# Attention software pipeline one unit deeper, bias and gate passes on GpSimd, and a second MLP that ends in token order with its residual in the accumulators

## The chip, the cores and the metric

The kernel runs on one core of a Trainium2 chip. The metric is the device time of one execution in microseconds, taken as the median of the runs shown. The profile comes from one further execution, whose span runs from its first to its last instruction.

## The reference, cut to what matters

One sequence of 256 tokens with width 1024 passes through two blocks. The first has gated linear attention, a sliding-window attention with eight heads (swa), an output product and an expert layer (PEER). The second has two layers. Only the parts around the change are shown:

```python
h = rmsnorm(x, g_attn[0]); x = x + dsa_mixer(h, rel_bias, ...)   # 8 heads, keys chosen by an indexer
x = x + sq_relu_mlp(rmsnorm(x, g_mlp[0]), w_up[0], w_down[0])
kv_shared = shared_kv(x, ...)
h = rmsnorm(x, g_attn[1]); x = x + nsa_mixer(h, rel_bias, kv_shared, ...)  # 8 heads, 3 gated branches
x = x + sq_relu_mlp(rmsnorm(x, g_mlp[1]), w_up[1], w_down[1])
return rmsnorm(x, g_final)

def sq_relu_mlp(h, w_up, w_down):                 # 1024 -> 4096 -> 1024
    return jnp.square(jax.nn.relu(h @ w_up)) @ w_down
```

In `dsa_mixer` the logits of a head are scores plus a relative bias plus a mask of the chosen keys. In `nsa_mixer` the softmax rows of the second and the third branch are multiplied by a sigmoid gate per token, head and branch before they meet the values.

## The kernel before, in words

**Layout.** Activations are held transposed: feature chunks of 128 on the partitions, 256 tokens along the free dimension (`XT`, eight chunks). Weights come as 488 slots of 128 x 1024 fp32 (512 KB each) through a ring of four, which SP refills when `slots_used` says that a slot is free (L369 to L374). Most slots are used in a split form: ScalarE writes a rounded high part (`split_high`, L337 to L343), VectorE or GpSimd the remainder into the slot's own place (`split_low`, L345 to L351), and a product is three fp32r matmuls, high x high, high x low and low x high (`three`, L525 to L529).

**The attentions.** `attention_units` (L94 to L99) lists 16 units for swa, 16 for dsa and 32 for nsa (two branches a head). Units of the first token tile (`tt` = 0) have 128 keys, those of the second 256. Each engine has its own `attend`, an in-order program over steps. TensorE in a step issues `scores(step)`, `transposes(step - 2)`, `products(step - 3)` (L634 to L640; L606, L615, L631). ScalarE issues `exps(st)`, `copies(st - 2)`, `outs(st - 4)` (L1064 to L1070). VectorE issues `logits(st)` (bias add and row maximum, L1407 and L1410) and then `normed(st - 1)` (reciprocal L1415 and a scaling L1419, in nsa with the gate, L1421). The buffers hold four units of scores and probabilities (`u % 4`) and two of transposed probabilities and of outputs (`u % 2`). For dsa the bias is two adds in a row on VectorE, the second waiting for the first: the relative bias `Bt` (L1834), then the mask `selb` (L1835). GpSimd does nothing in these stages, but for memsets (L422) and weight loads beside swa. In swa VectorE also has a filler, a row of the modulation of 128 x 1024 (L1442), in every second step.

**What comes between two score products.** `products(u)` waits for `att_copied` of its own unit and for `att_out` of the output two before it. Both are set by ScalarE in the iteration before, behind that iteration's `exps`, and `exps` waits for the row maximum of its own unit.

**The MLPs.** `mlp` (L897 to L915) works in rounds of eight slots: four up slots (L531; 24 matmuls of 128 x 256 into `pu`), which VectorE evacuates with relu (L1850) and ScalarE squares, then four down slots (`down_slot`, L567; 24 matmuls with the weights as the stationary side, 256 tokens moving, into `pacc`). The accumulators are opened by eight small matmuls with zeros (`open_acc`, L811), and closed in the same way (`close_acc`, L817). The expert layer's value product uses another form, `token_slot` (L576 to L587): the activations are stationary and 512 columns of weights move, 12 matmuls for a slot (L584 to L586), tokens on the partitions.

**The head of the second MLP.** Its first slot (`raw_slot`, L543) runs on the unnormalised stream. The sum of squares is made by GpSimd (L465) and TensorE (L558), ScalarE takes the root, VectorE the reciprocal (L1588), and only then can relu free the two `pu` entries.

**The tail.** After the last down slot: `close_acc`, the residual add on VectorE over 128 x 2048 (L1971), squares on ScalarE, a sum over the partitions by eight fp32 matmuls (`norm_sum("fin2")`, L517), root, reciprocal over 128 x 256 (L1392), eight scalings (L1394), and one store of 1 MB (L377), whose landing ends the kernel. Output leaves in feature order.

## Time and profile before

| | us |
|---|---|
| runs shown | 1850.57, 1854.89, 1855.41 |
| median | 1854.89 |
| profiled execution, its own time | 1855.27 |
| span of that execution | 1853.7 |
| TensorE busy | 1682.4 (91% of the span) |
| VectorE busy | 1069.6 (58%) |
| ScalarE busy | 835.0 (45%) |
| GpSimd busy | 448.0 (24%) |
| mean granted TensorE clock | 0.935 of full speed |

Matmul records are pipelined and their ends modelled, so neighbouring records overlap: the pace is the distance of their starts. A matmul with fp32 operands stands as two records (passes). In timeline rows the first number is the start, the second the length of a run of equal instructions, and the brackets hold the idle time before it and what ended that. Nearly all activations of ScalarE stand under L1006, a helper.

### The profile page before, as it was taken

The numbers are of one execution on the slowest core, as the hardware profiler recorded it, in microseconds if no ns is written. First come the engines' busy times: TensorE is split into PE (matmuls) and PEld (weight loads), VectorE is DVE, ScalarE is ACT, GpSimd is POOL, SyncE is SP. The second block draws the span as 40 slices with busy tenths as digits, with TensorE's granted clock in tenths as the row PEclk, the third lists the DMA queues.
The fourth block names the chain that finished last, engine by engine and source line by source line (L and its number), as shares of the span: only waits on it lengthen the run. The fifth ranks groups of instructions, "written<-read, shape, count | busy, mean of one in ns | idle before, by whom it ended". The sixth has DMA issues, their size and how long they took to land.

```text
span 1853.7 us, 34170 instructions
## 1 busy us (share of the span) xinstructions
PE 1682.4 (91%) x11384; PEld 1517.6 (82%) x11384; DVE 1069.6 (58%) x2448; ACT 835.0 (45%) x1767; POOL 448.0 (24%) x399
## 2 busy tenths in 40 slices
PE   5975889999999999999999977589999988899996
PEld 3872789998999999778887755479999848699996
DVE  5537569916777732555555542666555624765554
ACT  3214445565444445555555531355555403555553
POOL 4102367886666677000000010000000000010000
PEclk8975899999999999999999987699999987999999
DMA  8851234553444445555555531125555462045552
GB/s 312 326 187 46 78 128 149 178 177 127 141 136 138 145 159 181 192 190 190 190 191 191 191 128 46 45 81 170 182 182 182 145 216 91 1 154 183 184 182 91
DMA packets 80752, 287.63 MB, mean 155 GB/s; under 512 B 10080, under 2 KB 11408, under 8 KB 80432
## 3 DMA queue, kind: packets, MB, share of 16 engines
q1 hardware_dynamic: 72016, 257.30, 42.0%
q0 software_dynamic: 7344, 26.35, 3.8%
q10 hardware_dynamic: 1328, 3.15, 0.5%
q8 instruction: 38, 0.62, 0.1%
q14 instruction: 26, 0.21, 0.0%
HBM read 284.14 MB, written 2.62 MB: 155 GB/s over the span
## 4 chain that ended last, share of the span: by engine, by line
PE 83%; DVE 9%; ACT 3%; issue 2%; DMA 2%; POOL 1%; SPq 0%; DVEq 0%; ACTq 0%; POOLq 0%
PE pu L527 12%; PE pu L528 12%; PE pu L529 12%; PE pacc L586 6%; PE pacc L584 6%; PE pacc L585 6%; PE pacc L527 3%; PE pacc L528 3%; PE pacc L529 3%; PE pu L499 3%; PE pu L509 2%; PE pacc L631 2%; PE pm L800 2%; PE pn L800 2%; PE pn L517 1%
## 5 line engine op out<-in xcount | busy, mean ns | idle before, releaser
L343 ACT ACTIVATE ring_hi<-ring 128x512 fp32r<-128x512 f32 x880 | 505.6, 622 | 524.6 <-PE pu L529 288.1
L350 DVE TENSOR_TENSOR ring_lo<-ring,ring_hi 128x512 fp32r<-128x512 f32 x592 | 386.0, 694 | 336.4 <-ACT ring_hi L343 336.2
L527 PE MATMUL pu<-Xh,ring_hi 128*128 128x256 f32 x1472 | 431.0, 293 | 23.7 <-DVE Xl L1382 5.3
L528 PE MATMUL pu<-Xl,ring_hi 128*128 128x256 f32 x1472 | 419.6, 285 | 0.0
L529 PE MATMUL pu<-Xh,ring_lo 128*128 128x256 f32 x1472 | 419.3, 285 | 0.0
L350 POOL TENSOR_TENSOR ring_lo<-ring,ring_hi 128x512 fp32r<-128x512 f32 x288 | 370.2, 1307 | 130.8 <-ACT ring_hi L343 130.1
L527 PEld LDWEIGHTS pu<-Xh,ring_hi 128*128 128x128 f32 x1472 | 285.1, 194 | 30.2 <-issue 18.1
L528 PEld LDWEIGHTS pu<-Xl,ring_hi 128*128 128x128 f32 x1472 | 285.8, 194 | 0.2
L529 PEld LDWEIGHTS pu<-Xh,ring_lo 128*128 128x128 f32 x1472 | 285.2, 194 | 0.0
L584 PE MATMUL pacc<-ring_hi,vh 128*128 128x512 f32 x512 | 200.5, 392 | 0.0
L586 PE MATMUL pacc<-ring_lo,vh 128*128 128x512 f32 x512 | 200.5, 392 | 0.0
L585 PE MATMUL pacc<-ring_hi,vl 128*128 128x512 f32 x512 | 199.7, 390 | 0.0
L527 PE MATMUL pu<-X2h,ring_hi 128*128 128x256 f32 x512 | 145.8, 285 | 2.7 <-DVE big L1850 2.7
L527 PE MATMUL pacc<-act_h,ring_hi 128*128 128x256 f32 x512 | 144.9, 283 | 0.0
L528 PE MATMUL pacc<-act_l,ring_hi 128*128 128x256 f32 x512 | 144.9, 283 | 0.0
L529 PE MATMUL pacc<-act_h,ring_lo 128*128 128x256 f32 x512 | 144.9, 283 | 0.0
L528 PE MATMUL pu<-X2l,ring_hi 128*128 128x256 f32 x512 | 144.9, 283 | 0.0
L529 PE MATMUL pu<-X2h,ring_lo 128*128 128x256 f32 x512 | 144.8, 283 | 0.0
L584 PEld LDWEIGHTS pacc<-ring_hi,vh 128*128 128x128 f32 x512 | 96.0, 187 | 33.1 <-issue 5.5
L586 PEld LDWEIGHTS pacc<-ring_lo,vh 128*128 128x128 f32 x512 | 96.1, 188 | 21.1
L585 PEld LDWEIGHTS pacc<-ring_hi,vl 128*128 128x128 f32 x512 | 96.3, 188 | 16.1
L465 POOL TENSOR_TENSOR R<-sq 128x256 f32<-128x256 f32 x2 | 1.5, 744 | 430.0 <-ACT sq L1006 430.0
(328 smaller groups left out, 2619.0 us busy)
## 6 DMA issues: line engine op xcount, KB each, us to landing
ring<-in_weights SPq DMA_DIRECT2D x488, 512.0 KB, 3.3
big<-in_ada POOLq DMA_DIRECT2D x40, 512.0 KB, 6.2
bias_row<-big ACTq DMA_DIRECT2D x1, 1536.0 KB, 6.8
XT<-in_xT ACTq DMA_DIRECT2D x1, 1024.0 KB, 8.4
scr<-in_ada POOLq DMA_DIRECT2D x2, 512.0 KB, 12.4
tk<-in_ada POOLq DMA_DIRECT2D x2, 512.0 KB, 14.1
early_h<-in_ada POOLq DMA_DIRECT2D x2, 512.0 KB, 16.2
early_l<-in_ada POOLq DMA_DIRECT2D x2, 512.0 KB, 17.7
```

The source lines that it names most:

```text
L343: nc.scalar.activation(ring_hi[:, n % 2, half], ring[:, n % RING, half], ACT.Copy).then_inc(s["split_hi"], 1)
L350: api.tensor_tensor(ring_lo[:, n % RING, half], ring[:, n % RING, half], ring_hi[:, n % 2, half], ALU.subtract).then_inc(s[LOW[name][0]], 1)
L499: last = mm(entry(e), slot(n)[:, c * P:(c + 1) * P], rhs[:, c, :], start=(c == 0), stop=(c == C - 1))
L509: last = mm(entry(e)[:, tt * P:(tt + 1) * P], lhs[:, c, tt * P:(tt + 1) * P], slot(n)[:, c * P:(c + 1) * P], start=(c == 0), stop=(c == C ...
L527: mm(out, ring_hi[:, n % 2, w], xh, start=start, stop=False, skip_group_check=True)
L528: mm(out, ring_hi[:, n % 2, w], xl, start=False, stop=False, skip_group_check=True)
L529: return mm(out, ring_lo[:, n % RING, w], xh, start=False, stop=stop, skip_group_check=True)
L584: mm(out, xh[:, rows], ring_hi[:, n % 2, w], start=False, stop=False, skip_group_check=True)
L585: mm(out, xl[:, rows], ring_hi[:, n % 2, w], start=False, stop=False, skip_group_check=True)
L586: last = mm(out, xh[:, rows], ring_lo[:, n % RING, w], start=False, stop=False, skip_group_check=True)
L631: last = mm(out, v, p, start=(k == 0 and UNITS[u][4]), stop=(k == len(pairs) - 1 and UNITS[u][5]))
L800: last = mm((pm, pn)[k % 2][:, i * P:(i + 1) * P], sq[:, j // 2, j % 2 * P:(j % 2 + 1) * P], scr[:, j * P:(j + 1) * P], start=True, stop=True)
```

## The change

1. TensorE issues transposes three and products four units behind the scores; ScalarE's copies and outputs move by one step too. This holds for all three attentions.
2. dsa: GpSimd adds `Bt` and `selb` into the score buffer ahead of time (16 adds, up to four units ahead), and VectorE then has one add in place of two.
3. nsa: GpSimd multiplies the 32 probability tiles by reciprocal and gate; VectorE only makes the reciprocal.
4. Second MLP: down slots run as `token_slot`. In place of `open_acc`, 16 fp32 matmuls of 128 x 128 against the identity (`residual_rows`) bring the residual stream into the accumulators in token order, after the fourth up slot. The last slot finishes token tile 0 before token tile 1; there is no `close_acc`.
5. Tail: per token tile one Square with a row sum, a root of 128 x 1, a reciprocal of 128 x 1, two scalings of 128 x 512 against the gain row, and a store of 256 KB for each half. `norm_sum("fin2")` is gone. The gain row is loaded by GpSimd's queue (512 KB, one row to all partitions) at the start of the second MLP.

```diff
@@ sync
-            sp.wait_ge(s["out_ready"], 1)
-            sp.dma_start(out_d, sq[:, :, :].rearrange("p a b -> p (a b)")).then_inc(s["out_stored"], 16)
-            sp.wait_ge(s["out_stored"], 16)
+            for i in range(2 * TT):
+                sp.wait_ge(s["out_ready"], i + 1)
+                sp.dma_start(out_d[:, i * 512:(i + 1) * 512], out_rows[:, i // 2, i % 2 * 512:(i % 2 + 1) * 512])\
+                    .then_inc(s["out_stored"], 16)
+            sp.wait_ge(s["out_stored"], 16 * 2 * TT)
@@ gpsimd
+            u0, u1 = SPAN["dsa"]
+            for u in range(u0, u1):
+                tt, h = UNITS[u][1:3]
+                L = keys_of(u)
+                pool.wait_ge(s["chosen"], tt + 1)
+                if u >= u0 + 4:
+                    pool.wait_ge(s["att_exp"], u - 3)
+                nc.gpsimd.tensor_tensor(Sb[:, u % 4, 0:L], Bt[:, h, T - L:T], selb[:, tt, 0:L], ALU.add)\
+                    .then_inc(s["att_prebias"], 1)
             add_squares("mlp0")
+            pool.wait_ge(s["gates_done"], 1)
+            for u in range(*SPAN["nsa"]):
+                _, tt, h, b = UNITS[u][:4]
+                pool.wait_ge(s["att_inverse"], u + 1 - SPAN["nsa"][0])
+                pr = Pb[:, u % 4, 0:keys_of(u)]
+                nc.gpsimd.tensor_scalar(pr, pr, stats[:, 8 + u % 4:9 + u % 4], gates[:, tt, 3 * h + 1 + b:3 * h + 2 + b],
+                                        ALU.mult, ALU.mult).then_inc(s["att_normed"], 1)
             add_squares("mlp1")
+            pool.wait_ge(s["slots_used"], SLOT["mlp1"])
+            pool.dma_start(fin_row[:, :], fin_row_d.partition_broadcast(P)).then_inc(s["weights_row_loaded"], 16)
@@ tensor, attend
-                for step in range(u0, u1 + 3):
+                for step in range(u0, u1 + 4):
                     if step < u1:
                         scores(step)
-                    if u0 <= step - 2 < u1:
-                        transposes(step - 2)
                     if u0 <= step - 3 < u1:
-                        products(step - 3)
+                        transposes(step - 3)
+                    if u0 <= step - 4 < u1:
+                        products(step - 4)
@@ tensor, mlp
+            def down(name, k, g):
+                done = 0 if name == "mlp0" else FF // P
+                pe.wait_ge(s["act_tiles"], tick(g, 4, done + k // BODY * 4 + k % 4 + 1))
+                if name == "mlp0":
+                    down_slot(name, k, act_h[:, k % 4, :], act_l[:, k % 4, :], g)
+                else:
+                    token_slot(name, k, act_h[:, k % 4, :], act_l[:, k % 4, :], g)
+            def residual_rows(product):
+                for c in range(C):
+                    pe.wait_ge(s["evacs"], USE[product] + c + 1)
+                    for tt in range(TT):
+                        at0 = tt * D + c * P
+                        mm(paccf[:, at0:at0 + P], XT[:, c, tt * P:(tt + 1) * P], ident[:, :], start=(c % 4 == 0), stop=False,
+                           skip_group_check=True)
+            def last_rows(name, k):
+                n = SLOT[name] + k
+                for tt in range(TT):
+                    rows = slice(tt * P, (tt + 1) * P)
+                    xh, xl = act_h[:, k % 4, rows], act_l[:, k % 4, rows]
+                    for half, w in enumerate(halves):
+                        out = paccf[:, tt * D + half * 512:tt * D + (half + 1) * 512]
+                        split_ready(name, k, half, None)
+                        mm(out, xh, ring_hi[:, n % 2, w], start=False, stop=False, skip_group_check=True)
+                        mm(out, xl, ring_hi[:, n % 2, w], start=False, stop=False, skip_group_check=True)
+                        last = mm(out, xh, ring_lo[:, n % RING, w], start=False, stop=True, skip_group_check=True)
+                    last.then_inc(s["rows_done"], 1)
             def mlp(name):
-                open_acc()
...
+                if name == "mlp0":
+                    open_acc()
                 raw_slot(name, lambda c: None)
                 one_sum(name)
                 for k in range(1, 4):
                     up_slot(name, k, USE[name] + k, None, 4, None, raw_x[name])
-                four_down(None)
-                with pe.Fori(1, FF // P // 4) as g:
+                if name == "mlp1":
+                    residual_rows("b_o")
+                for k in range(4, 8):
+                    down(name, k, None)
+                with pe.Fori(1, FF // P // 4 - (name == "mlp1")) as g:
...
+                    for k in range(k0 + 4, k0 + 7):
+                        down(name, k, None)
+                    pe.wait_ge(s["act_tiles"], 2 * FF // P)
+                    last_rows(name, k0 + 7)
...
-            norm_sum("fin2")
@@ scalar, attend
-                for st in range(u0, u1 + 4):
+                for st in range(u0, u1 + 5):
                     if st < u1:
                         exps(st)
-                    if u0 <= st - 2 < u1:
-                        copies(st - 2)
-                    if u0 <= st - 4 < u1:
-                        outs(st - 4)
+                    if u0 <= st - 3 < u1:
+                        copies(st - 3)
+                    if u0 <= st - 5 < u1:
+                        outs(st - 5)
@@ scalar, tail
-            act.wait_ge(s["x_ready"], 4)
-            squares(XT[:, :, :], sq[:, :, :])
-            root(NORM["fin2"])
+            act.wait_ge(s["roots"], NORM["mlp1"])
+            for tt in range(TT):
+                act.wait_ge(s["rows_done"], tt + 1)
+                f(scratch[:, tt, :], paccf[:, tt * D:(tt + 1) * D], ACT.Square,
+                  accum_out=stats[:, tt:tt + 1]).then_inc(s["row_squares"], 1)
+                act.wait_ge(s["row_squares"], tt + 1)
+                f(stats[:, 4 + tt:5 + tt], stats[:, tt:tt + 1], ACT.Sqrt, scale=1.0 / D, bias=eps[:, 0:1])\
+                    .then_inc(s["row_roots"], 1)
@@ vector
+                    inverse = v.reciprocal(stats[:, 8 + u % 4:9 + u % 4], stats[:, 4 + u % 4:5 + u % 4])
+                    if kind == "nsa":
+                        inverse.then_inc(s["att_inverse"], 1)
+                        return
...
             def dsa_bias(u, S, ps):
-                step(v.tensor_tensor(S, ps, Bt[:, h, T - L:T], ALU.add))
-                v.tensor_tensor(S, S, selb[:, tt, 0:L], ALU.add).then_inc(s["att_biased"], 1)
+                dve.wait_ge(s["att_prebias"], u - SPAN["dsa"][0] + 1)
+                v.tensor_tensor(S, ps, S, ALU.add).then_inc(s["att_biased"], 1)
...
-            dve.wait_ge(s["acc_done"], 3)
-            v.tensor_tensor(XT[:, :, :], pacc[:, :, :], XT[:, :, :], ALU.add).then_inc(s["x_ready"], 1)
-            dve.wait_ge(s["x_ready"], 4)
-            scaled(sq, XT, [column("fin2", c) for c in range(C)], NORM["fin2"]).then_inc(s["out_ready"], 1)
+            def rows_out(tt):
+                dve.wait_ge(s["row_roots"], tt + 1)
+                step(v.reciprocal(stats[:, 8 + tt:9 + tt], stats[:, 4 + tt:5 + tt]))
+                for half in halves:
+                    v.scalar_tensor_tensor(out_rows[:, tt, half], paccf[:, tt * D + half.start:tt * D + half.stop],
+                                           stats[:, 8 + tt:9 + tt], fin_row[:, half], ALU.mult, ALU.mult)\
+                        .then_inc(s["out_ready"], 1)
+            dve.wait_ge(s["weights_row_loaded"], 16)
+            rows_out(0)
+            rows_out(1)
```

## Rows read from the trace of the kernel before

**Rows 1.** The page, part 4: shares of the chain that ended last.

```profile
PE 83%; DVE 9%; ACT 3%; issue 2%; DMA 2%; POOL 1%; SPq 0%; DVEq 0%; ACTq 0%; POOLq 0%
```

**Rows 2.** Windows (span; busy PE, PEld, DVE, ACT, POOL; PEclk; DMA): swa, second MLP.

```profile
160.00:198.00 38.00, 33.85 (x98) 17.74 (x98) 30.70 (x100) 16.61 (x65) 10.34 (x13) 0.52 0.17 56
...
1660.00:1833.00 173.00, 173.00 (x1444) 173.00 (x1442) 96.55 (x179) 86.53 (x178) 0.00 (x0) 1.00 0.53 174
```

**Rows 3.** Timeline of the tail.

```profile
1833.04 1.05 PE L817 MATMUL pacc<-zeros 128*128 128x256 bf16 x8
1834.13 2.29 DVE L1971 TENSOR_TENSOR XT<-pacc,XT 128x2048 f32<-128x2048 f32 x1 [4.63 <-PE pacc L817]
1836.45 1.91 ACT L1006 ACTIVATE sq<-XT 128x2048 f32<-128x2048 f32 x1 [7.76 <-DVE XT L1971]
1838.41 5.29 PE L517 MATMUL pn<-sq,ones 128*128 128x256 f32 x16 [4.33 <-ACT sq L1006]
...
1846.11 3.26 DVE L1394 SCALAR_TENSOR_TENSOR sq<-XT,cols,R 128x256 f32<-128x256 f32 x8
1849.39 0.36 SPq L377 DMA_DIRECT2D outT<-sq  x1
```

**Rows 4.** DMA issues (KB each, us from issue to landing): the store, and a small load.

```profile
big<-bias_row POOLq DMA_DIRECT2D x8, 128.0 KB, 2.4
...
outT<-sq SPq DMA_DIRECT2D x1, 1024.0 KB, 3.9
```

**Rows 5.** Line L584, token-order product (ns min/median/max, first and last start).

```profile
L584 PE MATMUL pacc<-ring_hi,vh x512: 387/389/474, 735.3 to 1086.1; 128*128 128x512 f32 x171
```

**Rows 6.** Timeline of TensorE, end of nsa: ten fp32 passes of 128 x 128.

```profile
1616.82 1.35 PE L631 MATMUL pacc<-big 128*128 128x128 f32 x10
```

**Rows 7.** Timeline of the head of the second MLP.

```profile
1648.74 1.28 ACT L1006 ACT_TABLE_LOAD   x1
...
1654.32 0.39 PE L527 MATMUL pu<-X2h,ring_hi 128*128 128x256 f32 x1 [1.35 <-DVE big L1850]
```

**Rows 8.** Timeline of TensorE in nsa, 256 keys, two steps.

```profile
1602.56 0.60 PE L606 MATMUL pm<-big 128*128 128x256 f32 x2
...
1604.64 0.44 PE L615 MATMUL pacc<-ident,big 128*128 128x128 f32 x2 [0.39 <-DVE big L1421]
...
1605.02 0.74 PEld L631 LDWEIGHTS pacc<-big 128*128 128x128 f32 x6 [0.18 <-ACT big L1006]
...
1605.80 0.60 PE L606 MATMUL pu<-big 128*128 128x256 f32 x2
```

**Rows 9.** The same with 128 keys: the score products at either end.

```profile
1582.94 0.39 PE L606 MATMUL pu<-big 128*128 128x128 f32 x2
...
1585.27 0.39 PE L606 MATMUL pm<-big 128*128 128x128 f32 x2
```

**Rows 10.** dsa: timeline of TensorE with 256 keys, and line L1835.

```profile
1210.64 0.60 PE L606 MATMUL pm<-big 128*128 128x256 f32 x2
...
1213.82 0.68 PE L631 MATMUL pacc<-big 128*128 128x128 f32 x4 [0.26 <-ACT big L1006]
...
1214.34 0.60 PE L606 MATMUL pu<-big 128*128 128x256 f32 x2
...
L1835 DVE TENSOR_TENSOR big<-big x16: 291/358/426, 1192.0 to 1217.1; 128x128 f32<-128x128 f32 x8, 128x256 f32<-128x256 f32 x8
```

**Rows 11.** Lines on GpSimd, and the scaling L1419 on VectorE (ns min/median/max).

```profile
L465 POOL TENSOR_TENSOR R<-R,sq x12: 734/739/745, 1238.9 to 1647.8; 128x256 f32<-128x256 f32 x12
...
L350 POOL TENSOR_TENSOR ring_lo<-ring,ring_hi x288: 1263/1294/2990, 232.0 to 731.0; 128x512 fp32r<-128x512 f32 x144
...
L1419 DVE TENSOR_SCALAR big<-big,stats x32: 285/353/1119, 161.8 to 1218.9; 128x128 f32<-128x128 f32 x16, 128x256 f32<-128x256 f32 x16
```

**Rows 12.** Timeline of swa beside GpSimd's memsets.

```profile
180.97 0.69 PE L615 MATMUL pacc<-ident,big 128*128 128x128 f32 x2 [0.50 <-DVE big L1419]
...
181.86 1.10 DVE L1419 TENSOR_SCALAR big<-big,stats 128x256 f32<-128x256 f32 x1
```

More of the change, by code:

```diff
@@ L192, in build @@
         ssum = R[:, T:2 * T]
+        fin_row = sb("fin_row", [P, D], F32, where["Xh"])
+        scratch = sb("scratch", [P, TT, D], F32, where["Xl"])
+        out_rows = sb("out_rows", [P, TT, D], F32, where["sq"])
         def area_r(name, *dims):
@@ L909, in mlp @@
                     up_slot(name, k, USE[name] + k, None, 4, None, raw_x[name])
-                four_down(None)
-                with pe.Fori(1, FF // P // 4) as g:
+                if name == "mlp1":
[3 more added lines that the diff above has]
+                with pe.Fori(1, FF // P // 4 - (name == "mlp1")) as g:
                     for k in range(4):
                         up_slot(name, k, USE[name] + k, g, 4, None, raw_x[name])
-                    four_down(g)
-                close_acc()
+                    for k in range(4, 8):
+                        down(name, k, g)
+                if name == "mlp0":
+                    close_acc()
+                else:
+                    k0 = 2 * FF // P - BODY
+                    for k in range(k0, k0 + 4):
+                        up_slot(name, k, USE[name] + k // BODY * 4 + k % 4, None, 4, None, raw_x[name])
+                    for k in range(k0 + 4, k0 + 7):
+                        down(name, k, None)
+                    pe.wait_ge(s["act_tiles"], 2 * FF // P)
+                    last_rows(name, k0 + 7)
             mlp("mlp0")
@@ L1395, in scaled, with attend @@
                 return last
-            def attend(kind, bias, gate=None, filler=None):
+            def attend(kind, bias, filler=None):
                 u0, u1 = SPAN[kind]
@@ L1826, in _ @@
                 L = (tt + 1) * P
-                last = v.tensor_scalar(selb[:, tt, 0:L], work[:, tt, 0:L], -2.0e38, NEG, ALU.is_gt, ALU.mult)
-            step(last)
-            dve.wait_ge(s["bias_ready"], 1)
+                v.tensor_scalar(selb[:, tt, 0:L], work[:, tt, 0:L], -2.0e38, NEG, ALU.is_gt, ALU.mult)\
+                    .then_inc(s["chosen"], 1)
             def dsa_bias(u, S, ps):
@@ L1934, in _ @@
             step(v.tensor_scalar(gates, gates, 1.0, None, ALU.add))
-            step(v.reciprocal(gates, gates))
+            v.reciprocal(gates, gates).then_inc(s["gates_done"], 1)
+            dve.wait_ge(s["gates_done"], 1)
             dve.wait_ge(s["cmp_psum"], 1)
@@ L1964, in _ @@
             split_low(dve, v, "b_o", 1)
[L1965 to L1966 removed]
+            attend("nsa", nsa_bias)
             both_low("b_o", oT)
```

28 lines of the change are left out of this document (8 added, 20 removed).

## The prediction

> **What bounds the kernel now.** I read the chain of waits first: TensorE holds 83% of what ended last, VectorE 9% [rows 1]. So engine shares say little, and each changed stage has to be read alone. The windows give the first split [rows 2]. In the second MLP TensorE is busy for all 173.0 of 173.0 us at full clock, so there the number and pace of matmuls is the time. In swa it is busy 33.9 of 38 us at a granted clock of 0.52, near its lower level of 1.2 GHz, so swa is close to TensorE-bound too. The timelines of nsa and dsa show another picture: TensorE stands still twice in each pair of steps [rows 8, 10]. The tail is a plain chain, one engine after another, from the last down product to the store [rows 3].
>
> **The tail.** Before: the closing matmuls start at 1833.04, where the last product's issue ends (its modelled end is some 0.2 us later, 1833.2), and the span ends at 1853.7, 20.5 us on. After: ScalarE squares 128x1024 with a row sum. The 128x2048 squares took 1.91 [rows 3], so half, 0.96, plus 0.2 for reading the sum and the wait: 1.2. The square of token tile 0 runs beside the six products of tile 1 and delays this by 0.1. The root of 128x1 and its waits: 0.3 (small instructions are bounded by 0.1 and 0.5, the length of the 128x256 ones; I take the middle). Reciprocal of 128x1 with waits: 0.3, same bounds. Two scalings of 128x512: eight of 128x256 took 3.26, so 0.41 each [rows 3], and twice that, less a fixed part, is 0.7 to 0.8; two are 1.5. The store: 1 MB landed 3.9 after its issue, a 128 KB load 2.4 [rows 4]; a 256 KB piece lies nearer the small one, 2.7, and the end came 0.4 after landing. Sum: 1.2 + 0.1 + 0.3 + 0.3 + 1.5 + 2.7 + 0.4 = 6.5 us. Gain **14.0** (bounds 12.5 to 15: a landing of 3.9 at one end, 2.4 and the short small steps at the other). The three earlier pieces lie beside the scalings.
>
> **The down slots.** A feature-order slot is 24 matmuls. In the 173.0 us of the second MLP's window stand 1444 of them, 0.120 each without a gap, so a slot is 2.88 [rows 2]. The token form exists in the expert layer: 128 slots from 735.3 to 1086.8 are 2.746 each [rows 5], loop gaps included. 32 slots x 0.134 = **4.3** gained (bounds: 0, if another feeder sets the pace, and 4.9). ScalarE and VectorE split the same bytes as in the expert layer and were half idle there and here.
>
> **The residual in the accumulators.** 16 matmuls of 128x128 in fp32 are 32 passes. Ten such passes took 1.35 including the last one's modelled end [rows 6], so 0.12 each in a row: 3.8. They stand before the first down product, where TensorE has no wait: the head's only wait is 1.35 before the third up slot [rows 7], and the residual comes after the fourth. Nothing covers it: I take **3.7** lost (bounds 3.4, and 7.4 at the lower clock). The opening matmuls that it replaces took about 1.05, like the closing ones [rows 3], but removing them gains only 0.1: the third up slot waits for relu, relu for the reciprocal, and that for a root behind a table load that ends at 1650.02 whatever TensorE does [rows 7]. The wait of 1.35 grows instead. The gain row's 512 KB load by GpSimd goes out in this head; nobody waits for it until the tail. It runs beside ring loads while the DMA engines are busy 53% [rows 2]: 0, bound 1 lost.
>
> **The deeper pipeline.** Follow one pair of steps in nsa. Scores at 1602.56; two VectorE steps, the exponential and ScalarE's copy follow; the products of the next step start at 1605.02, released by ScalarE, and take until 1605.80, where the next scores start [rows 8]. So S(n+1) = S(n-1) + 2.46 + 0.78 = 3.24 for two steps. TensorE also waited at 1604.64 for VectorE's scaling, but its two transposes, at some 0.12 a pass, were done before 1604.9, ahead of 1605.02: this wait is hidden by the one behind it. The change moves transposes, copies and products all by one. Products(st-4) then need the copy that ScalarE makes in iteration st-1, behind exps(st-1): the very relation that products(st-3) have now. The binding loop holds no depth that grows. So the wait on the scaling goes and the wait on ScalarE grows by as much. With 128 keys a pair takes 2.33 [rows 9] in the same loop. nsa: **0** from depth. At the fill one score product goes earlier, at the drain one more step follows; ±1.
>
> In swa the rows differ: TensorE waited 0.50 for a scaling that a memset of GpSimd had stretched [rows 12], and one score product leaves a TensorE-bound stretch at the fill (about 0.6 at the low clock). I take **1.0** gained (0 to 2).
>
> **nsa's gate pass on GpSimd.** VectorE's scaling is not in the loop above, so taking it away gains nothing. GpSimd's version adds latency between reciprocal and transposes. Its price is in no row. Bounds: a two-input add of the same size, 0.74, and the slowest GpSimd row, 2.99 for twice the elements [rows 11]; below, VectorE's own 0.41. I take 0.74, the nearest. The transposes have a step more, 1.2 to 1.6 us, and the pass had taken 0.41: up to about 1.5 is covered, and also fits once per unit in 1.62. Cost **0**.
> The Trainium skill (GPSIMD Engine Reference, Engine selection) says that GpSimd is about half as fast as VectorE with two inputs and roughly at line rate with one; no row here shows the second. By it the pass would cost about what VectorE's does, an estimate, and the sum would not change.
>
> **dsa.** The loop is the same with a second add in it: scores 1210.64, products 1213.82, next scores 1214.34, 3.70 for two steps [rows 10]. The second add (0.29 and 0.43 in the two tiles; with its wait 0.32 and 0.46) leaves the loop once in two steps: 4 x 0.32 + 4 x 0.46 = 3.1 gained. GpSimd's add of 0.74 [rows 11] starts at the exponential's end and has until VectorE's next add for that buffer, four steps: covered. But at the start four of them meet VectorE's remainders for the first `a_o` slot, and every one may meet the scaling L1419. The rows show what that meeting costs: L1419 of 128x256 took 1.10 beside a GpSimd memset against a median of 0.35 [rows 11, 12]. In the steady loop the scaling follows a row maximum directly, and GpSimd's add only the end of the exponential which that maximum released, an estimated 0.6 later; with 0.74 it is over before the next scaling, a step of 1.62 on. So only the start pays: 0.6, about one add. dsa gains **2.5** (0 to 4).
> The Trainium skill (SBUF — State Buffer, Who interferes with whom) says that a VectorE instruction in a two-port mode, or with two SBUF inputs against a GpSimd one that reads SBUF, and a GpSimd instruction exclude each other for their whole length, whoever starts first. The trace agrees for L1419 (1.10). If that befell every unit, it would be the rival below.
>
> **Sum.** 14.0 + 4.3 - 3.7 + 0.1 + 1.0 + 0 + 2.5 = 18.2 us. The profiled execution took 1855.27, 0.4 over the median of the runs; 1855.27 - 18.2 = 1837.1, and on the median's level **1836.7**.
>
> **Rivals.**
> - *The attentions do speed up with depth.* If the products did not wait for the exponential of the step before, nsa would run at TensorE's own pace. Its waits are 0.39 and 0.18 of a pair by the records [rows 8], up to 0.8 by the starts; 0.4 less per unit over 32 units is at most 12 to 13 more, 1824. For it: TensorE waits for VectorE's scaling in each pair [rows 8]. Against: the wait right behind it.
> - *Port meetings in dsa.* L1419 at 1.1 instead of 0.35 in each unit puts 0.75 on VectorE where the second add took 0.3 to 0.46 off: dsa gains nothing, 1839 to 1840. For it: rows 12.
> - *The second MLP pays more.* The down slots stay at 2.88, or the identity matmuls run at the low clock: 4 more each, 1841 with one of them.
> - *Slower.* GpSimd's gate pass is far dearer than its add. Place: 32 units of nsa; it decides above 1.62 with 256 keys and 1.17 with 128. At 2.99 a pass, the slowest GpSimd row [rows 11], nsa takes 32 x 3.05 = 98 in place of 46, and the kernel comes to about 1889. It eats the whole gain from about 2.0 a unit. Against: 0.74 for a two-input add.
> - *The deepening does not do what it says* is part of my forecast already: nothing hangs on it.
>
> **How the numbers follow.** Forecast as summed: 0.60. Faster attentions 0.08. Port meetings 0.14. Dearer MLP 0.13. Slow gate pass 0.03; the remaining 0.02 is disorder of the granted clock, which in dsa and nsa is at its lower level for part of the time. The forecast's own spread is 1832 to 1841 from the bounds of tail, residual and swa. The range takes in port meetings and the dearer MLP, and on the low side part of the faster attentions: 1830 to 1843. A difference of under 0.3% (5.6 us) can't be told from none in this kernel. All cases but the slow gate pass are faster by more: 0.96, same 0.02, slower 0.02.
>
> **What the profile after would show.** In the tail: some 6.5 us from the last product to the end, a store piece landing in under 3. In the second MLP: down slots at 2.75, and 3.7 of identity matmuls with no wait before them; a larger wait than 1.35 before the third up slot. In nsa: pairs still 3.24 and 2.33, TensorE waiting for ScalarE alone, and by 0.4 or so. In dsa: pairs of 3.24 in place of 3.70. I am wrong if nsa shrinks by several us, if L1419 is stretched in steady dsa, or if GpSimd's gate pass is over 1.2.

## The result, and the profile after

| | us |
|---|---|
| changed kernel, four runs | 1831.44, 1833.68, 1835.06, 1837.62; median 1834.37 |
| kernel before, four runs beside it | 1850.57, 1851.15, 1854.89, 1855.41; median 1853.02 |
| ratio | 0.9897, 95% interval 0.9877 to 0.9918 |
| profiled execution | 1835.06, span 1833.5 (before 1855.27, span 1853.7) |
| forecast | 1836.7, range 1830 to 1843, faster |

The page's chain has hardly moved: TensorE 82% for 83%, VectorE 8% for 9% [rows 1]. A change worth 1% isn't read there. I cut both traces at the same events (an instruction with one tile shape, found in each trace); the differences, in us:

| stage, by its first and last event | before | after | forecast of the change |
|---|---|---|---|
| start to swa's first scores | 146.20 | 144.80 | 0 |
| swa, to the first product of the output weights | 60.62 | 60.93 | -1.0 |
| from there to the expert layer's accumulators | 527.68 | 529.03 | 0 |
| expert layer | 352.33 | 352.20 | 0 |
| to the last replace (L1889) of dsa's choice | 102.69 | 101.29 | 0 |
| dsa, from that replace to the first MLP's opening matmuls | 63.37 | 60.45 | -2.5 |
| first MLP | 187.27 | 187.27 | 0 |
| shared keys, to the last transposes of the compressed branch | 126.77 | 125.66 | 0 |
| nsa, to the first split of its result | 51.59 | 51.39 | 0 |
| second output product, to the sum of squares | 31.00 | 31.71 | 0 |
| head of the second MLP, to the first down slot | 10.72 | 14.66 | +3.6 |
| to the issue end of the last product | 172.80 | 167.95 | -4.3 |
| tail | 20.66 | 6.16 | -14.0 |

The tail, from the timeline of the changed kernel (start, length, engine, line):

```profile
1827.11 0.39 PE L950 MATMUL pacc<-ring_lo,act_h 128*128 128x512 f32 x1
1827.59 1.00 ACT L1068 ACTIVATE scratch<-pacc 128x1024 f32<-128x1024 f32 x1
1828.49 0.19 ACT L1068 ACTIVATION_READ_ACCUMULATOR scratch<-pacc 128x1 f32 x1
1828.71 0.29 ACT L1068 ACTIVATE stats<-stats,eps 128x1 f32<-128x1 f32 x1
1829.31 0.15 DVE L2038 RECIPROCAL stats<-stats 128x1 f32<-128x1 f32 x1
1829.50 1.41 DVE L2040 SCALAR_TENSOR_TENSOR out_rows<-pacc,stats,fin_row 128x512 f32<-128x512 f32 x2
```

The reader sees token tile 1 alone: square at 1827.59, root at 1828.71, reciprocal at 1829.31, and the two scalings end at 1830.91, 2.6 before the span's end. In the kernel before 20.7 us lay between the issue end of the last product and the end [rows 3]. Tile 1's reciprocal waited 0.3 for VectorE, which was still scaling tile 0. The head and the steady part of the second MLP:

```profile
1644.52 1.28 ACT L1068 ACT_TABLE_LOAD   x1
1649.99 0.38 PE L551 MATMUL pu<-X2h,ring_hi 128*128 128x256 f32 x1 [1.81 <-DVE big L1915]
1655.90 3.74 PE L936 MATMUL pacc<-ident,XT 128*128 128x128 f32 x32
1659.39 0.47 PE L608 MATMUL pacc<-ring_hi,act_h 128*128 128x512 f32 x1
```

The wait before the third up slot grew from 1.35 [rows 7] to 1.81, and the 32 passes of the residual follow the fourth up slot without a gap: 3.49 from their start to the next matmul. The window over the rest (busy us and count for each engine, granted clock, DMA share, GB/s):

```profile
1655.00:1827.00 172.00, 172.00 (x1096) 156.90 (x1096) 97.18 (x180) 87.38 (x179) 0.00 (x0) 1.00 0.54 176
```

TensorE is as full as before [rows 2]: the gain there is shorter work. A down slot is 12 matmuls 0.227 apart, 2.72.

nsa with 256 keys, TensorE alone:

```profile
1597.47 0.60 PE L630 MATMUL pn<-big 128*128 128x256 f32 x2
1597.90 0.38 PE L639 MATMUL pacc<-ident,big 128*128 128x128 f32 x2
1598.12 0.61 PE L655 MATMUL pacc<-big 128*128 128x128 f32 x4
1598.57 0.60 PE L630 MATMUL pu<-big 128*128 128x256 f32 x2
1599.94 0.94 PE L655 MATMUL pacc<-big 128*128 128x128 f32 x6 [0.56 <-ACT big L1068]
1600.71 0.60 PE L630 MATMUL pu<-big 128*128 128x256 f32 x2
```

The pair is 1600.71 - 1597.47 = 3.24, to the hundredth what it was [rows 8]. Of the two waits of before, 0.39 and 0.18, only the one for ScalarE is left, and it is 0.56: the time moved from one wait to the other. dsa:

```profile
1206.90 0.60 PE L630 MATMUL pn<-big 128*128 128x256 f32 x2
1208.19 0.60 PE L630 MATMUL pu<-big 128*128 128x256 f32 x2
1209.63 0.68 PE L655 MATMUL pacc<-big 128*128 128x128 f32 x4 [0.63 <-ACT big L1068]
1210.15 0.60 PE L630 MATMUL pu<-big 128*128 128x256 f32 x2
```

A pair is 3.25 where it was 3.70 [rows 10]: one add fewer in the same loop. The stage of the table also holds the output product behind dsa, the same code in both kernels. Its windows, before and after (columns as above):

```profile
1228.10:1252.89 24.79, 24.30 (x192) 23.38 (x193) 16.36 (x29) 13.58 (x30) 4.44 (x6) 1.00 0.47 155
1222.41:1248.70 26.29, 25.76 (x192) 24.84 (x193) 16.36 (x29) 13.57 (x30) 4.46 (x6) 0.94 0.44 149
```

It is 1.5 us longer after, with the granted clock at 0.94 in place of 1.00. So the 2.9 gained in the stage are 4.5 in dsa's steps (27.69 and 23.21 from the first transposes to the last product) less 1.5 behind them. In the steps the granted clock was 0.71 before and 0.87 after, so part of the 4.5 may be the clock's. GpSimd's groups, by form (busy, mean ns):

```profile
L500 POOL TENSOR_SCALAR big<-big,stats 128x256 f32<-128x256 f32 x16 | 8.9, 558 | 16.1 <-DVE stats L1482 16.1
L500 POOL TENSOR_SCALAR big<-big,stats 128x128 f32<-128x128 f32 x16 | 7.2, 451 | 326.5 <-DVE stats L1482 326.4
L492 POOL TENSOR_TENSOR big<-big 128x256 f32<-128x256 f32 x8 | 5.8, 725 | 5.7 <-ACT big L1068 5.7
```

The gate pass is 0.56, less than the 0.74 I took.

### The profile page after: what moved, and what is told of

The parts are those of the page before. It is cut to its first block, busy times and chain, and to the rows that moved or that the text cites. A ratio compares the mean times of both kernels' runs of the same rounds, so it can differ in the third digit from the quotient of the medians.

```text
span 1833.5 us, 33401 instructions
## 1 busy us (share of the span) xinstructions
PE 1665.3 (91%) x11000; PEld 1493.6 (81%) x11000; DVE 1049.1 (57%) x2396; ACT 835.8 (46%) x1771; POOL 475.4 (26%) x448
## 4 chain that ended last, share of the span: by engine, by line
PE 82%; DVE 8%; ACT 4%; issue 3%; DMA 2%; POOL 1%; SPq 0%; DVEq 0%; ACTq 0%; POOLq 0%
PE pu L551 12%; PE pu L552 11%; PE pu L553 11%; PE pacc L608 8%; PE pacc L610 8%; PE pacc L609 8%; PE pu L523 3%; PE pacc L655 2%; PE pu L533 2%; PE pacc L552 2%; PE pacc L551 2%; PE pacc L553 2%; PE pn L824 2%; PE pm L824 2%; ACT big L1068 1%
## 5 line engine op out<-in xcount | busy, mean ns | idle before, releaser
L500 POOL TENSOR_SCALAR big<-big,stats 128x128 f32<-128x128 f32 (+1 forms) x32 | 16.1, 504 | 342.6 <-DVE stats L1482 342.5
L551 PEld LDWEIGHTS pu<-X2h,ring_hi 128*128 128x128 f32 x512 | 98.2, 192 | 4.2 <-DVE big L1915 3.6
L552 PEld LDWEIGHTS pu<-X2l,ring_hi 128*128 128x128 f32 x512 | 98.2, 192 | 0.3
L553 PEld LDWEIGHTS pu<-X2h,ring_lo 128*128 128x128 f32 x512 | 98.2, 192 | 0.0
```

What stands on the lines that cost most here:

```text
L551: mm(out, ring_hi[:, n % 2, w], xh, start=start, stop=False, skip_group_check=True)
L552: mm(out, ring_hi[:, n % 2, w], xl, start=False, stop=False, skip_group_check=True)
L553: return mm(out, ring_lo[:, n % RING, w], xh, start=False, stop=stop, skip_group_check=True)
```

## The experiments

Each kernel was timed against the kernel before on the same chip. Ratios are given where several runs were made; a stage is read from one profile of each kernel.

**1. The second MLP and the tail alone.** All attentions as in the kernel before, so against the changed kernel:

```diff
-                for step in range(u0, u1 + 4):
+                for step in range(u0, u1 + 3):
...
-                nc.gpsimd.tensor_tensor(Sb[:, u % 4, 0:L], Bt[:, h, T - L:T], selb[:, tt, 0:L], ALU.add)\
-                    .then_inc(s["att_prebias"], 1)
...
-                nc.gpsimd.tensor_scalar(pr, pr, stats[:, 8 + u % 4:9 + u % 4], gates[:, tt, 3 * h + 1 + b:3 * h + 2 + b],
-                                        ALU.mult, ALU.mult).then_inc(s["att_normed"], 1)
```

> The second MLP and the tail as in the changed kernel, all three attentions as before. Theory: they carry the gain. By the terms of the prediction 14.0 (tail) + 4.3 (down slots) - 3.7 (residual) + 0.1 = 14.7 us, so a ratio of 0.992 against the kernel before (0.9915 to 0.9925), some 1838 to 1839 us. Rival, the attentions gave much of it: under 12 us here, ratio above 0.9935. In its profile the attention stages last as before: nsa from the last transposes of the compressed branch to the first split of its result 51.6 us, dsa from the last choice mask to the opening matmuls of the first MLP 62.9 us.

Measured: 0.9901, 0.9885 to 0.9916 (18.4 us of 1855.6). The profile shows nsa 51.62 and dsa 63.36 (by the events of the table, which for dsa lie 0.5 earlier than the one in the expectation), and from the sum of squares to the span's end 188.75 against 204.18, so 15.4 us: 14.7 was forecast. The other 3 lie in stages that the edit doesn't touch. The ratio is a little under the 0.9915 to 0.9925 expected. This part carries the result, and the attentions' 3 us are about as large as what unchanged stages vary by.

**2. The depth alone**, in the kernel before.

> The kernel before with the deeper pipeline alone (transposes three, products four units behind, ScalarE's copies and outputs one step later), in all three attentions. Theory: the loop of two steps runs through ScalarE, whose copy for products(st-4) stands behind exps(st-1) as it did for products(st-3), so depth gives nothing: nsa 51.6 +-1, dsa 62.9 +-1, swa 60.6 +-1, total within 2 us of before, ratio 0.999 to 1.001; pairs of steps stay at 3.24 (nsa, 256 keys) and 3.70 (dsa). Rival, VectorE's scaling was the wait that counted: nsa shrinks by 0.4 for each of 32 units, 12 us, ratio 0.993.

```diff
-                for step in range(u0, u1 + 3):
+                for step in range(u0, u1 + 4):
...
-                    if u0 <= step - 2 < u1:
-                        transposes(step - 2)
-                    if u0 <= step - 3 < u1:
-                        products(step - 3)
+                    if u0 <= step - 3 < u1:
+                        transposes(step - 3)
+                    if u0 <= step - 4 < u1:
+                        products(step - 4)
...
```

Measured: 0.9994, 0.9983 to 1.0006; nsa 52.12, dsa 64.06, swa 58.74. The steady pairs stay at 3.24 and 3.71: depth is worth nothing by itself. nsa is 0.5 longer, for one more step at the drain: its last product ends 5.5 behind the last scores in place of 4.8. The 0.7 of dsa are something else: the steps took 26.91 in place of 27.69, and the output product behind them 26.26 in place of 24.79, at the lower clock that the changed kernel had there too.

**3. ScalarE's copies and outputs ahead of its exponentials**, in the changed kernel.

```diff
-                    if st < u1:
-                        exps(st)
                     if u0 <= st - 3 < u1:
                         copies(st - 3)
                     if u0 <= st - 5 < u1:
                         outs(st - 5)
+                    if st < u1:
+                        exps(st)
```

> The changed kernel, and in each step ScalarE issues copies(st-3) and outs(st-5) ahead of exps(st) instead of behind it. Theory: the loop that set 3.24 us for a pair of steps is products(st-4) waiting for the copy and the output behind exps(st-1). With that order turned, the loop spans three units (scores to exponential 1.6, exponential 0.7, copy and output 0.5, products and scores 0.8, together 3.6), 1.2 us a unit; each engine's own work is about 1.1 a unit. So nsa's units of 256 keys go from 1.62 to 1.2 or 1.3 and those of 128 from 1.17 to about 0.9: nsa 51.4 to about 41, dsa 3 to 4 less, swa (TensorE-bound at the low clock) the same to 1 less. Total 11 to 15 us under the changed kernel, about 1821, ratio to before 0.982 to 0.984. Rival, the pace is set by an engine's own throughput or by VectorE's chain: under 3 us, ratio above 0.988.

Measured: 0.9790, 0.9771 to 0.9809. nsa 39.74, dsa 56.39. TensorE in nsa, and under it the window of that stretch:

```profile
1587.81 0.60 PE L630 MATMUL pm<-big 128*128 128x256 f32 x2
1588.24 0.38 PE L639 MATMUL pacc<-ident,big 128*128 128x128 f32 x2
1588.46 0.83 PE L655 MATMUL pacc<-big 128*128 128x128 f32 x6
1589.13 0.60 PE L630 MATMUL pn<-big 128*128 128x256 f32 x2
1590.23 0.60 PE L630 MATMUL pu<-big 128*128 128x256 f32 x2
```

```profile
1588.00:1601.00 13.00, 12.93 (x98) 11.71 (x97) 7.77 (x27) 10.05 (x35) 5.54 (x10) 1.00 0.01 3
```

The waits are gone, the pair is 1590.23 - 1587.81 = 2.42 in place of 3.24, and TensorE is busy 12.93 of 13.00 us where it had been 10.55 in the same window before this edit. Two lines in another place are worth 15.7 us in nsa and dsa by the profile, as much as the whole MLP part. swa gained as well: from the first scores to the last product it took 49.6 in place of 51.8. All three are more than I expected, and so is the total (0.982 to 0.984 expected).

**4. The same order, with the old depth.** As 3, but transposes two and products three units behind.

```diff
...
-                for st in range(u0, u1 + 5):
-                    if st < u1:
-                        exps(st)
-                    if u0 <= st - 3 < u1:
-                        copies(st - 3)
-                    if u0 <= st - 5 < u1:
-                        outs(st - 5)
+                for st in range(u0, u1 + 4):
+                    if u0 <= st - 2 < u1:
+                        copies(st - 2)
+                    if u0 <= st - 4 < u1:
+                        outs(st - 4)
+                    if st < u1:
+                        exps(st)
```

> As copies_first, but with the depth of the kernel before (transposes two, products three units behind, copies(st-2), outs(st-4), exps(st)). Theory: the order on ScalarE makes the gain, not the depth. A unit's loop over three units then runs scores, two VectorE steps 1.6, exponential 0.7, reciprocal and gate pass on GpSimd 0.9, transposes and products 0.9, about 4.0 or 1.35 a unit against TensorE's own 1.21: nsa 40 to 42.5, dsa within 1 of 56.4, total 0 to 3 us over copies_first, ratio 0.979 to 0.981. Rival, the depth is what made room: nsa 46 or more.

Measured: 0.9882, 0.9861 to 0.9903; nsa 51.07, dsa 57.20. My expectation fell, and the rival held for nsa (dsa came within 1 us of experiment 3, as expected). The timeline:

```profile
1590.09 0.42 DVE L2027 TENSOR_TENSOR big<-pm,big 128x256 f32<-128x256 f32 x1 [1.19 <-PE pm L630]
1590.55 0.42 DVE L1477 TENSOR_REDUCE stats<-big 128x1 f32<-128x256 f32 x1
1590.89 0.15 DVE L1482 RECIPROCAL stats<-stats 128x1 f32<-128x1 f32 x1
1591.14 0.55 POOL L500 TENSOR_SCALAR big<-big,stats 128x256 f32<-128x256 f32 x1 [1.58 <-DVE stats L1482]
1591.75 0.44 PE L639 MATMUL pacc<-ident,big 128*128 128x128 f32 x2 [0.59 <-POOL big L500]
1592.02 0.83 PE L655 MATMUL pacc<-big 128*128 128x128 f32 x6
1592.69 0.60 PE L630 MATMUL pu<-big 128*128 128x256 f32 x2
```

There is a second loop of two units. VectorE makes the reciprocal of st-1 only behind the maximum of st; then come gate pass, transposes, products and scores(st+2). The add at 1590.09 belongs to scores that start at 1589.45, and from there to the scores at 1592.69 it is again 3.24. The kernel before has this loop too; its wait is the one that I had called hidden. Depth widens this one to three units; the order on ScalarE takes the exponential out of the other. Either alone leaves the other loop in force.

**5. The order alone**, in the kernel before, where the scaling and the gate pass are VectorE's.

```diff
-                    if st < u1:
-                        exps(st)
                     if u0 <= st - 2 < u1:
                         copies(st - 2)
                     if u0 <= st - 4 < u1:
                         outs(st - 4)
+                    if st < u1:
+                        exps(st)
```

> The kernel before with ScalarE's order alone (copies(st-2), outs(st-4), exps(st)); its depth, its two adds in dsa and its gate pass on VectorE stay. My theory that order alone makes the gain fell with shallow_copies_first (nsa 51.1, with TensorE waiting for GpSimd's gate pass). New theory: there are two loops of two units. One runs through ScalarE's order. The other is scores(st), add and maximum of st, reciprocal and scaling of st-1 behind them on VectorE, transposes(st-1), products, scores(st+2); in shallow_copies_first it is 0.64 + 0.45 + 0.34 + 0.25 + 0.55 + 0.05 + 0.28 + 0.67 = 3.23 for two units, the gate pass on GpSimd included. With the scaling on VectorE it is 0.35 shorter, 2.9: nsa's pairs of 256 keys fall from 3.24 to 2.9, nsa from 51.6 to 46 to 48; dsa with both adds in the loop 3.3 for 3.70, from 63.4 to 60 to 62. Total 5 to 8 us under before, ratio 0.9955 to 0.9975. Rival, depth is needed whatever stands in the loop: nsa 51 or more, ratio above 0.998.

Measured: 0.9962, 0.9948 to 0.9975 (7 us); nsa 48.27, dsa 59.85. TensorE in nsa:

```profile
1590.00 0.60 PE L606 MATMUL pu<-big 128*128 128x256 f32 x2
1591.10 0.60 PE L606 MATMUL pu<-big 128*128 128x256 f32 x2
1592.09 0.44 PE L615 MATMUL pacc<-ident,big 128*128 128x128 f32 x2 [0.39 <-DVE big L1421]
1593.03 0.60 PE L606 MATMUL pm<-big 128*128 128x256 f32 x2
```

A pair of 3.03 (2.9 expected), and the wait is for VectorE. nsa is 0.3 above the range expected and dsa just below its own. The second loop's length is set by what stands in it: 3.03 with the scaling on VectorE, 3.24 with the pass on GpSimd. So at the old depth with this order, moving the gate pass costs nsa 2.8 us (48.27 to 51.07).

**6. Only the copy ahead**: copies, exps, outs.

```diff
-                    if st < u1:
-                        exps(st)
                     if u0 <= st - 3 < u1:
                         copies(st - 3)
+                    if st < u1:
+                        exps(st)
                     if u0 <= st - 5 < u1:
                         outs(st - 5)
```

> As copies_first, but in each step of ScalarE copies(st-3), exps(st), outs(st-5): only the copy stands ahead of the exponential. Theory: products(u) waits for its copy and for the output two outputs before. In dsa each unit is an output, so products(u) waits for outs(u-2), which stands behind exps(u+3) again, the old loop: dsa back at about 60.5, pairs of 3.25 with 256 keys. In nsa an output ends only with every second unit, and the one needed was made one or two steps earlier: nsa stays at 39.7 +-1. Rival, what counts is only that the copy goes first: dsa 56.4 too.

Measured in one run: 1819.53; nsa 40.24 and dsa 56.91, not 60.5. The loop is there, its price was wrong:

```profile
1200.84 0.60 PE L630 MATMUL pu<-big 128*128 128x256 f32 x2
1202.32 0.60 PE L630 MATMUL pm<-big 128*128 128x256 f32 x2
1203.30 0.68 PE L655 MATMUL pacc<-big 128*128 128x128 f32 x4 [0.16 <-ACT big L1068]
1203.82 0.60 PE L630 MATMUL pn<-big 128*128 128x256 f32 x2
```

A pair is 2.98, between 3.25 and the 2.5 to 2.8 of experiment 3: of ScalarE's two instructions the copy has left the loop and the output has not. The 56.91 flatters, since the output product behind the steps ran at full clock here (24.79) and not in the changed kernel or in experiment 3 (26.29, 26.27). From the first transposes to the last product dsa took 23.21 in the changed kernel, 21.16 here and 19.17 in experiment 3. So half of what the order gains in dsa needs the output ahead of the exponential too; neither my theory nor the rival holds. nsa, where an output ends with every second unit, doesn't notice, as expected.

**7. The gate pass back on VectorE**, otherwise as 3.

```diff
-                nc.gpsimd.tensor_scalar(pr, pr, stats[:, 8 + u % 4:9 + u % 4], gates[:, tt, 3 * h + 1 + b:3 * h + 2 + b],
-                                        ALU.mult, ALU.mult).then_inc(s["att_normed"], 1)
...
+                        last = v.tensor_scalar(pr, pr, stats[:, 8 + u % 4:9 + u % 4], gate(u), ALU.mult, ALU.mult)
```

> As copies_first, but the gate pass of nsa is back on VectorE. Theory: in the changed kernel the pass was beside the loop and its place worth nothing; with the loop open, VectorE's add, maximum, reciprocal and scaling come to about 1.35 a unit with 256 keys (0.9 + 0.1 + 0.35) against TensorE's 1.21, and 1.1 against 0.9 with 128: nsa 42 to 45 instead of 39.7. Rival, VectorE still has room: 39.7 +-0.7.

Measured in one run: 1823.44; nsa 43.91. In the changed kernel the place of this pass was worth nothing; with both loops open it is worth 4.2 us, since VectorE's own work in a unit (starts 1.30 apart, busy 8.51 of the 9.00 us from 1585 to 1594) is then longer than TensorE's 1.21.

**8 and 9. GpSimd's part made longer**, in the changed kernel, by one and by two more passes over the same tile:

```diff
+                nc.gpsimd.tensor_scalar(pr, pr, 1.0, None, ALU.mult).then_inc(s["gate_pass"], 1)
+                pool.wait_ge(s["gate_pass"], ...)
```

> The changed kernel with GpSimd's gate pass preceded by one more pass over the same tile (a product with 1.0), so that GpSimd's part of a unit doubles. Theory: the pass (0.56 with 256 keys, 0.45 with 128) stands beside the loop; two passes and their waits are 1.4 and 1.2 a unit against periods of 1.62 and 1.17: nsa 51.4 to 53. Rival, GpSimd's latency is already in the loop: each unit 0.4 to 0.6 longer, nsa 64 or more.

> The same with two more passes, three in all. Theory: now GpSimd is the bound, about 2.0 a unit with 256 keys and 1.6 to 1.7 with 128: nsa 16 x 2.0 + 16 x 1.65 = 58 and a few us of fill, 58 to 63, against 51.4. Rival, the cover ends later (more than 1.5 us, the figure of the prediction, is hidden): nsa under 55.

Measured in one run each: nsa 52.57 and 73.75. The added pass is dearer than the gate pass (kernel with three passes, 256 keys):

```profile
L500 POOL TENSOR_SCALAR big<-big 128x256 f32<-128x256 f32 x16 | 13.6, 848 | 0.0
L502 POOL TENSOR_SCALAR big<-big 128x256 f32<-128x256 f32 x16 | 13.6, 848 | 1.3
L504 POOL TENSOR_SCALAR big<-big,stats 128x256 f32<-128x256 f32 x16 | 8.9, 554 | 1.7
```

With two passes GpSimd's part is 0.85 + 0.55 and a wait of 0.1, just inside 1.62; the steady pairs stay at 3.24, and nsa pays 1.2 us at its ends. With three a unit takes 2.40 (the three rows and their waits) and nsa 22 us more. So of the cover of "up to about 1.5" in the prediction 1.5 is shown, and that it ends below 2.4. My 58 to 63 for three passes was too low: I had priced a pass by 0.56, which makes 6.4 us in 16 units of 0.4, and left too little for fill and drain, about 9. The run also bears out the forecast's slower case: at 2.40 and 1.66 a unit, 2.03 in the mean ("about 2.0" in the prediction), the gate pass alone takes the whole gain away (1858.62 against 1856.61 for the kernel before).

**10. The residual one place earlier**, in the changed kernel:

```diff
                 for k in range(1, 4):
+                    if name == "mlp1" and k == 2:
+                        residual_rows("b_o")
                     up_slot(name, k, USE[name] + k, None, 4, None, raw_x[name])
-                if name == "mlp1":
-                    residual_rows("b_o")
```

> The changed kernel with the 16 identity matmuls of the residual put ahead of the third up slot of the second MLP (after two up slots, not after four), where TensorE waits 1.81 us for relu. Theory: they take 3.74 us without a wait, of which 1.8 now stand in that wait: the wait goes, the third up slot starts 1.9 later and the first down slot 1.8 earlier; total 1.8 us under the changed kernel, ratio to before 0.0010 lower. Rival: what feeds the later slots (relu, the split of the ring) is late instead, and the wait shows up before the fourth up slot or the first down slot: no gain.

Measured: 0.9866, 0.9851 to 0.9881. By the profile the stretch from the sum of squares to the end is 186.63 against 188.77, so 2.1 us (1.8 expected); no wait stands behind the identity matmuls:

```profile
1644.17 3.74 PE L936 MATMUL pacc<-ident,XT 128*128 128x128 f32 x32
1647.66 0.36 PE L551 MATMUL pu<-X2h,ring_hi 128*128 128x256 f32 x1
```

The ratio fell by 0.0031, more than this part can give (0.0010 expected); the two intervals overlap, so only the profile's 2.1 us are shown.

**11. One store of 1 MB** in the changed kernel in place of four.

```diff
-            for i in range(2 * TT):
-                sp.wait_ge(s["out_ready"], i + 1)
-                sp.dma_start(out_d[:, i * 512:(i + 1) * 512], out_rows[:, i // 2, i % 2 * 512:(i % 2 + 1) * 512])\
-                    .then_inc(s["out_stored"], 16)
+            sp.wait_ge(s["out_ready"], 2 * TT)
+            sp.dma_start(out_d, out_rows[:, :, :].rearrange("p a b -> p (a b)")).then_inc(s["out_stored"], 16)
```

> The changed kernel with one store of 1 MB at the end in place of four of 256 KB. Theory: the last piece landed 2.5 us after the last scaling's store was issued; one store of 1 MB lands about 3.9 after its issue, as in the kernel before: from the start of the last product to the end of the span 7.8 to 8.2 us in place of 6.4. Rival, the last store's time is a fixed latency whatever its size: 6.4 to 6.8.

Measured in one run: the last product starts at 1823.65 and the span ends at 1831.7, 8.05; with four stores it is 1833.5 - 1827.11 = 6.39. Of the tail's gain 1.7 us are due to the cutting of the store, 12.8 to the shorter and the missing steps.

**12. Both edits together**, the diffs of 3 and 10 in the changed kernel.

> The changed kernel with both edits that helped: ScalarE's copies and outputs ahead of its exponentials, and the residual's matmuls ahead of the third up slot. Theory: the two lie in different stages and add: nsa 39.7, dsa 56.4, the second MLP's head 1.8 shorter. About 1813 to 1816 us, ratio to before 0.976 to 0.978. Rival, the gain of copies_first came partly from a better phase of the clock: nsa over 42, ratio 0.980 or more.

Measured: 0.9782, 0.9760 to 0.9804, median 1814.94 against 1853.69. nsa 40.05, dsa 56.24, and 186.54 from the sum of squares to the end. By their stages the two add (15.6 and 2.2 under the changed kernel), and this is the fastest version found: 39 us under the kernel before, twice the gain of the change. Its lead over experiment 3 is too small for the intervals.

## Why the prediction was right, and where not

The total came within 2.3 us (1836.7 against 1834.4). Of these, 1.9 are the level of the kernel before, which ran at 1853.02 beside the changed kernel and not at 1854.89; the difference of the two is 18.65 for 18.2 forecast. The terms one by one:

- **Tail**, 14.0 forecast, 14.5 measured. Squares and reading 1.12 with the wait (1.2 taken); root and reciprocal with theirs 0.79 (0.6); two scalings 1.41 (1.5). Experiment 11 confirms the price of the large store, 3.9 from issue to landing. The small one was mis-sized: the four pieces landed 2.2 after their issue (median), for 2.7 taken.
- **Down slots**, 4.3, measured 4.85: the slot is 2.72, a little under the 2.746 with loop gaps of the expert layer [rows 5].
- **Residual**, 3.7, measured 3.49, and the relu wait behind the table load grew as said (1.81). Together with the output product before it, in whose first microseconds the clock was lower than in the kernel before (granted 0.70 from 1616 to 1620 us, 1.00 before), the two stages paid 4.65 in this execution. In experiment 1, at full clock throughout, they took 45.10 for 41.72 before, so 3.4 (3.6 forecast). What I missed is that the wait of 1.35 which I named was free cover for the same matmuls; experiment 10 used it for 2.1 us.
- **dsa**, 2.5, measured 2.9. The pair fell to 3.25 as worked out, but that the stage agrees is partly luck: its steps gained 4.5 and the output product behind them lost 1.5, and the forecast had neither. How much of the 4.5 came with the higher clock in the steps stays open. The scaling L1488 took 0.31 and 0.35 in the mean, so the port meetings of the rival did not come in the steady steps. At the start they did: of the first four GpSimd adds of 128 keys two took 0.90 beside VectorE's remainders (all others 0.45), and the remainders 0.95 in place of 0.69. VectorE's first add then came 2.54 behind the last replace in place of 2.11, so 0.4 lost where the sum has 0.6.
- **nsa**, 0, measured 0.2. The loop over two units was read rightly, 3.24 before and after.
- **swa** is the step that failed: "I take **1.0** gained (0 to 2)". The profile shows 0.3 lost, 0.2 of it between the first scores and the last product (51.60 before, 51.78 after). I counted the score product that leaves at the fill and the wait for a stretched scaling, but not what takes their place. The rows of the changed kernel:

```profile
162.85 0.47 PE L639 MATMUL pacc<-ident,big 128*128 128x128 f32 x1 [0.92 <-DVE big L1488]
164.12 0.69 PE L655 MATMUL pacc<-big 128*64 128x128 f32 x2 [0.80 <-ACT big L1068]
166.24 0.69 PE L655 MATMUL pacc<-big 128*64 128x128 f32 x2 [0.30 <-ACT big L1068]
179.16 0.66 PE L655 MATMUL pacc<-big 128*64 128x128 f32 x2 [0.46 <-ACT big L1068]
```

  The first wait for VectorE is as in the kernel before (0.92). 0.80 and 0.30 are new, and 0.46 for ScalarE stands where 0.50 for the scaling was [rows 12]. The score product that left the fill comes back as a step at the drain: the last scores stand 44.0 behind the first in place of 45.5, but the last product ends 7.8 behind them in place of 6.1. This stretch repeats well: 51.5 to 51.6 in the four profiles at the old depth, 51.8 in four with the attentions of the change, and 51.0 in two more in which the clock rose 2 to 3 us earlier. With the copy ahead of the exponential at the new depth the 0.80 is gone, and it is 49.6 to 51.2. The rest of the stage varies by 1.7 us between the profiles, so the whole stage (59.3 to 60.6 at the old depth, 58.7 to 60.9 at the new) doesn't show the difference.
- **The step "the deeper pipeline"** holds as it stands, but it read only the longest of two loops. It followed that depth gives nothing here. It did not follow that depth is useless: with ScalarE's order turned and the gate pass on GpSimd, nsa is 51.07 at the old depth and 39.74 at the new one. The prediction even had the second loop's wait in hand ("this wait is hidden by the one behind it") and left its length unwritten.
- **The rivals.** Faster attentions did not occur, port meetings only at the start of dsa, and the dearer MLP neither. The rule of the Trainium skill (GPSIMD Engine Reference, Engine selection), roughly line rate with one input, fits the gate pass only roughly: 0.56, a third more than VectorE's 0.41 for the same tile. It doesn't fit the product with 1.0, 0.85.

The stages that the change touches are 18.2 us shorter in sum, which is the sum forecast. That it agrees to the tenth is luck: swa and the second MLP's head together fell 1.7 short of their terms, and tail, down slots, dsa and nsa were 1.7 over theirs. The other 2.0 of the 20.2 us between the two profiled executions lie in stages that it doesn't touch (-2.7 up to nsa, +0.7 in the output product).

## What to carry to other kernels

When engines run in-order programs over steps, write down every loop between the score products of two units, with its length and the number of units that it spans, not only the longest. A deeper pipeline pays only for loops that hold the distance it changes, and an edit to one loop shows nothing while another of equal length stands: here, of nsa's 51.6 us, depth alone gave nothing, ScalarE's order alone 3.3, both together 7.7 with the gate pass on VectorE and 11.9 with it on GpSimd. A stage that also holds unchanged code is cut once more before its time is given to the change: in dsa the output product hid 1.5 of the 2.0 us that experiment 6 lost against experiment 3. And whatever work is new on the bound engine should be tried in the waits that its profile already shows.

## What was not expected of the hardware

- A GpSimd multiplication of 128x256 by two per-partition operands took 0.55, by the immediate 1.0 alone 0.85 (128x128: 0.45 and 0.53).
- Stages of unchanged code moved by 1 to 2 us from one execution to the next, with the granted clock. From the expert layer's end to the reciprocal of 128x768 it was 56.0 to 58.1 in 14 profiles; in the slice 6 to 12 us behind that end the clock was granted at 0.61 in one and 0.77 in another. The output product behind dsa took 24.8 in four profiles, in which the clock was full, and 26.1 to 26.3 in ten, in which it was granted at half for 3.4 us around its start. So a term of 1 us outside the second MLP can't be confirmed by one profile.
